# A hybrid encoder step on one core: the order of work around its search and attention, and where modulation rows are made

## The reference

```python
# A: gMLP over chunks of 128 tokens
u, v = split(gelu(za)); v = group_standardize(v)
a = u * (tril(w_spatial) @ v + b_spatial)
# B: attention on the 256 best keys of an indexer
score = sum_h(wi[h] * relu(qi[h] @ ki.T)); keep = top_k(score, 256)
b = softmax(q @ k.T / 8, over keep) @ v       # 8 heads on 2 key heads
# C: gated convolution of width 31, standardize, silu
x = x + ga1 * (concat(a, b, c) @ w_out)
x = x + ga2 * ((silu(h2 @ w_gate) * (h2 @ w_up)) @ w_down)
```

## Time and profile before

| | |
|---|---|
| median of 3 runs | 3089.64 us (3088.87 to 3091.21) |
| profiled execution | 3094.46 us, span 3092.7 us, mean granted clock of TensorE 0.961 |
| TensorE, matmul | 2847.1 us busy (92%) |
| VectorE | 1653.3 us (53%) |
| ScalarE | 985.8 us (32%) |
| GpSimd | 617.6 us (20%) |
| DMA | 224.93 MB, mean 73 GB/s |

### The profile page before, as it was taken

How to read it: one execution, slowest core, us unless ns; L and a number is a source line. 1 busy time by engine, 2 the same in 40 slices (tenths; PEclk the granted TensorE clock), 3 DMA queues, 4 the chain that set the end, 5 groups by cost and what they waited for, 6 DMA issues and landing times.

```text
span 3092.7 us, 42630 instructions
## 1 busy us (share of the span) xinstructions
PE 2847.1 (92%) x15994; PEld 2459.7 (80%) x16018; DVE 1653.3 (53%) x2788; ACT 985.8 (32%) x1259; POOL 617.6 (20%) x262
## 2 busy tenths in 40 slices
PE   5999778969999999999979987889999999999996
PEld 2778633349999999999967875333899999999996
DVE  6758766684352443534544778564335435353355
ACT  4246536523221111111233563563332111111112
POOL 1411300001122222222242122000112222222221
PEclk9999889979999999999989998999899999999998
DMA  5412100142122222222241311001112222222222
GB/s 212 134 63 83 35 21 1 38 168 75 66 83 70 82 71 86 80 70 82 70 141 43 116 49 36 1 1 34 56 55 88 70 80 78 72 88 70 80 80 85
DMA packets 71351, 224.93 MB, mean 73 GB/s; under 512 B 17232, under 2 KB 17488, under 8 KB 70096
## 3 DMA queue, kind: packets, MB, share of 16 engines
q1 hardware_dynamic: 69664, 217.26, 21.1%
q10 hardware_dynamic: 1584, 6.29, 0.5%
HBM read 211.44 MB, written 11.54 MB: 72 GB/s over the span
## 4 chain that ended last, share of the span: by engine, by line
issue 46%; PE 36%; DVE 6%; ACT 5%; POOL 4%; DVEq 2%; DMA 1%; ACTq 0%; POOLq 0%; SPq 0%
PE ps L919 33%; ACT notsel L728 4%; POOL w_lo L581 4%; PE ps L965 1%; DVE hf L1311 1%; DMA w_ada<-in_w_ada 1%; DVEq L1436 1%; PE ps L1026 1%; DVE ada_later L1330 1%; DVE ada_junk L1330 0%; PE ps L945 0%; DVE s_cand L1434 0%; DVE swapped L1401 0%; DVEq L1340 0%; PE ps L903 0%
## 5 line engine op out<-in xcount | busy, mean ns | idle before, releaser
L581 POOL TENSOR_TENSOR w_lo<-w_raw,w_hi 128x1024 fp32r<-128x1024 f32 x202 | 498.3, 2467 | 2360.6 <-ACT w_hi L680 2360.6
L919 PE MATMUL ps<-u_hi,w_hi 128*128 128x352 f32 (+1 forms) x2112 | 457.4, 325 | 2.1 <-ACT rstd L872 2.1
L919 PE MATMUL ps<-u_hi,w_lo 128*128 128x352 f32 (+1 forms) x2112 | 458.4, 325 | 0.0
L919 PE MATMUL ps<-u_lo,w_hi 128*128 128x352 f32 (+1 forms) x2112 | 455.7, 324 | 0.0
L680 ACT CAST w_hi<-w_raw 128x1024 fp32r<-128x1024 f32 x202 | 211.0, 1045 | 545.7 <-PE ps L919 336.1
L919 PEld LDWEIGHTS ps<-u_hi,w_hi 128*128 128x128 f32 x2112 | 362.1, 189 | 3.7 <-ACT rstd L872 2.7
L919 PEld LDWEIGHTS ps<-u_hi,w_lo 128*128 128x128 f32 x2112 | 361.0, 189 | 0.0
L919 PEld LDWEIGHTS ps<-u_lo,w_hi 128*128 128x128 f32 x2112 | 361.0, 189 | 0.0
L728 ACT ACTIVATE notsel<-score,s_cand 128x384 bf16<-128x384 f32 (+3 forms) x248 | 297.4, 1200 | 142.2 <-DVE s_cand L1434 141.9
L1741 DVE SCALAR_TENSOR_TENSOR x<-ps,mod,x 128x704 f32 (+2 forms) x240 | 125.4, 578 | 364.5 <-PE ps L919 358.8
L919 PE MATMUL ps<-a_hi,w_hi 128*128 128x352 f32 x1056 | 228.8, 325 | 4.2 <-POOL w_lo L581 2.1
(11 more groups left out here) (260 smaller groups left out, 4122.9 us busy)
## 6 DMA issues: line engine op xcount, KB each, us to landing
w_ada<-in_w_ada SPq DMA_DIRECT2D x96, 512.0 KB, 4.6
w_raw<-in_w_up SPq DMA_DIRECT2D x88, 512.0 KB, 3.5
w_raw<-in_w_in SPq DMA_DIRECT2D x34, 512.0 KB, 3.6
ada_later<-in_w_ada SPq DMA_DIRECT2D x32, 512.0 KB, 3.5
cw<-in_convw SPq DMA_DIRECT2D x32, 512.0 KB, 4.5
w_raw<-in_w_down SPq DMA_DIRECT2D x32, 384.0 KB, 3.1
w_raw<-in_w_down SPq DMA_DIRECT2D x32, 320.0 KB, 2.9
w_raw<-in_w_out SPq DMA_DIRECT2D x16, 512.0 KB, 3.5
```

Of the source, the lines that this page charges most:

```text
L581: nc.gpsimd.tensor_tensor(w_lo[slot][:], w_raw[:], w_hi[slot][:].bitcast(F32), ALU.subtract)\
L919: last = nc.tensor.matmul(ps[:, bank + t, 0:w], wt[slot][:, kk, :], mv[:, kk, t * TW:t * TW + w], start=(kk == 0 and p == 0), stop=(kk == ...
```

## The change

At the start TensorE makes eight groups of modulation rows in place of twelve, VectorE eight in place of four; both of VectorE's loads are on SP's queue, TensorE's on ScalarE's. `ADA_AT` is 3, 3, 1, 3, ten in all, and the later part is twelve and ten; SP loads them three at a time. `pv` of a unit is issued behind the next unit of `ORDER`, whichever kind it is. In `SEARCH_BESIDE` rounds ScalarE's count stands behind the exponentials. ScalarE's `turned(0)` stands in front of the last prompt search round; VectorE has gate rows 0, then `q_samp`, then `finish_search`, gate rows 1, the last `scale`, and both selects. SP loads strip 18 (`FIRST_OUT + 1`) directly behind the cached values. `output(QB)` stands in front of `modulation(l, 1, 2, 6)`.

```diff
@@ -108,11 +108,11 @@
 TILE = TOK * 4
-ADA_PE, ADA_DVE = 3, 1
+ADA_PE, ADA_DVE = 2, 2
...
 ADA_SLOTS = 3
-ADA_AT = {0: 2, 1: 2, 2: 2, 3: 2}
+ADA_AT = {0: 3, 1: 3, 2: 1, 3: 3}
 ADA_STRIPS = sum(ADA_AT.values())
@@ -418,7 +418,9 @@
             sp.dma_start(cond_row[:], a["cond_row"]).then_inc(row_loaded.sem, 16)
-            sp.dma_start(w_ada0[0][:], a["w_ada"][DEPTH - 1, 4 * ADA_PE:ADA_FIRST].rearrange("m p k -> p m k")).then_inc(ada0_loaded[0].sem, 16)
+            for n in range(ADA_DVE):
+                m = 4 * (ADA_PE + n)
+                sp.dma_start(w_ada0[n][:], a["w_ada"][DEPTH - 1, m:m + 4].rearrange("m p k -> p m k")).then_inc(ada0_loaded[n].sem, 16)
@@ -466,7 +468,7 @@
                     if l == 0 and 3 <= j <= 5:
-                        load_later(2 * j - 3, min(2 * j - 1, ADA_STRIPS))
+                        load_later(3 * j - 6, min(3 * j - 3, ADA_STRIPS))
                     if j == S_QI1:
@@ -531,18 +533,18 @@
                     sp.dma_start(vcache[:, :, n, 0:HD], a["vcache"][l, :, :, n]).then_inc(kv_cached.sem, 16)
+                load_strip(FIRST_OUT + 1, a["w_out"][l, 1])
                 if l == 0:
...
                         bring_back(d)
-                for j in range(1, OUT_STRIPS):
+                sp.wait_ge(c_ready.sem, c_ready.at(l, 2))
+                settle(sp)
+                for d in range(4, KD):
+                    bring_back(d)
+                for j in range(2, OUT_STRIPS):
                     load_strip(FIRST_OUT + j, a["w_out"][l, j])
-                    if j == 1:
-                        sp.wait_ge(c_ready.sem, c_ready.at(l, 2))
-                        settle(sp)
-                        for d in range(4, KD):
-                            bring_back(d)
@@ -695,7 +697,8 @@
             for n in range(ADA_PE):
-                act.dma_start(w_ada0[1 + n][:], a["w_ada0"][4 * n:4 * n + 4].rearrange("m p k -> p m k")).then_inc(ada0_loaded[1 + n].sem, 16)
+                act.dma_start(w_ada0[ADA_DVE + n][:], a["w_ada0"][4 * n:4 * n + 4].rearrange("m p k -> p m k"))\
+                    .then_inc(ada0_loaded[ADA_DVE + n].sem, 16)
             act.wait_ge(consts_made.sem, 1)
@@ -747,6 +750,14 @@
                     last.then_inc(st_rstd.sem, 1)
+
+                def turned(m):
+
+                    act.wait_ge(vn_turned.sem, vn_turned.at(l, m + 1))
+                    if m == 1:
+                        act.wait_ge(sp_ready.sem, sp_ready.at(l, 1))
+                    nc.scalar.copy(vnat[:, 0:QB, :], ps[:, 6:8, :])
+                    nc.scalar.copy(vnat[0:DEC, QB, :], ps[0:DEC, 5, 0:P]).then_inc(vn_ready.sem, 1)
@@ -787,18 +798,15 @@
                         square_centred(STATS_IN[j + 1])
+                    if j == IN_STRIPS - 1:
+                        turned(0)
                     if j in SEARCH_AFTER:
...
-                for m in range(2):
-                    act.wait_ge(vn_turned.sem, vn_turned.at(l, m + 1))
-                    if m == 1:
-                        act.wait_ge(sp_ready.sem, sp_ready.at(l, 1))
-                    nc.scalar.copy(vnat[:, 0:QB, :], ps[:, 6:8, :])
-                    nc.scalar.copy(vnat[0:DEC, QB, :], ps[0:DEC, 5, 0:P]).then_inc(vn_ready.sem, 1)
+                turned(1)
                 act.wait_ge(vaug_ones.sem, vaug_ones.at(l, 1))
@@ -827,10 +835,10 @@
                             searched += 1
+                    exponentials(t, P, PLACE["S", t], 512)
                     if kb < SEARCH_BESIDE.get(i, 0):
...
                         searched += 1
-                    exponentials(t, P, PLACE["S", t], 512)
                     if kb == i:
@@ -938,12 +946,12 @@
             for n in range(ADA_PE):
-                pe.wait_ge(ada0_loaded[1 + n].sem, 16)
+                pe.wait_ge(ada0_loaded[ADA_DVE + n].sem, 16)
                 if n >= 2:
...
                     last = nc.tensor.matmul(ps[0:2, n % 2, :], cond[:, kk, :],
-                                            w_ada0[1 + n][:, :, kk * P:(kk + 1) * P],
+                                            w_ada0[ADA_DVE + n][:, :, kk * P:(kk + 1) * P],
                                             start=(kk == 0), stop=(kk == KD - 1))
@@ -1167,16 +1175,16 @@
+                late = None
                 for kind, n in ORDER:
...
                         logits(n)
-                        continue
-                    st(n)
-                    i, kb = S_UNITS[n]
-                    if kb >= 1:
-                        pv(n - 1)
-                    if kb == i:
-                        pv(n)
+                    else:
+                        st(n)
+                    if late is not None:
+                        pv(late)
+                    late = n if kind == "S" else None
+                pv(late)
@@ -1383,10 +1391,11 @@
-            dve.wait_ge(ada0_loaded[0].sem, 16)
-            for e in range(4):
-                modulate(w_ada0[0][:, e], 4 * ADA_PE + e)
-                dve.drain()
+            for n in range(ADA_DVE):
+                dve.wait_ge(ada0_loaded[n].sem, 16)
+                for e in range(4):
+                    modulate(w_ada0[n][:, e], 4 * (ADA_PE + n) + e)
+                    dve.drain()
             cos = cossin[:, 0, :]
@@ -1595,12 +1604,9 @@
                             nc.vector.tensor_copy(score[0:DEC, s0:s0 + w], ps[0:DEC, 7, 0:w]).then_inc(samp_taken.sem, 1)
-                    if j == S_Q3:
-                        dve.wait_ge(kv_rot.sem, kv_rot.at(l, 5))
-                        nc.vector.tensor_copy(q_samp[:].rearrange("p (b t) -> p b t", b=4), q[:, :, SEQ:TOK])
                     if j == 8:
                         turn_input(1)
-                    if j in STATS_IN:
+                    if j in STATS_IN and j < S_Q3:
                         scale(STATS_IN[j])
@@ -1616,11 +1622,7 @@
-                finish_search(0, PSRCH)
-
-                assert searched == BITS
-
-                for m in range(2):
+                def gate_rows(m):
@@ -1634,6 +1636,14 @@
                     nc.vector.tensor_tensor(mix[:, m, :], mix[:, m, :], gu[:, m, :], ALU.mult).then_inc(gated.sem, 1)
+
+                gate_rows(0)
+                dve.wait_ge(kv_rot.sem, kv_rot.at(l, 5))
+                nc.vector.tensor_copy(q_samp[:].rearrange("p (b t) -> p b t", b=4), q[:, :, SEQ:TOK])
+                finish_search(0, PSRCH)
+                gate_rows(1)
+                scale(STATS_IN[S_Q3])
+                for m in range(2):
                     select(m, rank).then_inc(sel_ready.sem, 1)
@@ -1709,7 +1719,7 @@
                         diagonals(i + 1)
-                half = ADA_STRIPS + (48 - ADA_FIRST - ADA_STRIPS) // 2
+                half = ADA_STRIPS + 12
                 output(QB - 2, 2, P, (QB - 2) * P, (QB - 1) * P)
@@ -1725,8 +1735,9 @@
                     modulate_later(half, 48 - ADA_FIRST)
+                output(QB, 3, DEC, SEQ, TOK)
+                if l == 0:
                     modulation(l, 1, 2, 6)
-                output(QB, 3, DEC, SEQ, TOK)
                 for kk in range(KD):
```

## The result

The changed kernel takes 3095.93 us (median, 3091.97 to 3098.53) where the kernel before took 3090.22 in the same comparison: a ratio of 1.0017, 95% interval 1.0009 to 1.0024, so 5.7 us slower. The forecast was 3095.4. Its traced execution, though, took 3091.97 us, the lowest of all its times, and that of the kernel before 3094.46, near its highest.

The account below looks back on a forecast made before the run. Feed-forward halves and later output strips keep TensorE above 99%; in attention it waits for exponentials beside the search chains. Terms -3.2 + 7.1 - 5.6 + 7.45 = +5.75, added to the median 3089.64, give 3095.4 us; range 3080 to 3106.

Parts of the forecast that it names:

- The start: Up to the first strip: TensorE loses its third group, VectorE gets four more rows, `hf` starts at 54.7; -3.2 us.
- The forecast collision: At the start: a VectorE row piece beside POOL's split takes 3.3 us instead of 1.2, so VectorE ends at 53.7.
- Ten rows: Layer 0's first strips: ten modulation rows instead of eight, strip 4's wait grows from 4.98 to 12 us; +7.1 us.
- The gate stage: Between last input strip and attention: no wait at `q_samp`, first `smax` at 405.4 instead of 408.25; -2.85 us per layer.
- Attention: Late sums queue behind `select`, delaying reciprocals and the next block's first count; +7.45 us per layer, gate stage's gain included.
- The low clock: In attention, behind waits before block 4's logits and block 7's scores: TensorE's clock falls, costing 2.7 and 1.5 us.
- Layer 0's end: Ten rows instead of twelve, strip 18 loaded early, `output(QB)` first: cast at 683.65 instead of 689.22; -5.6 us, attention included.
- Rival C: Attention: low clock behind both long waits in both layers, +8.95 and -4.1, sum +8.75, 3098.4 us; 27%.
- Rival B: Attention: no low clock at all, +3.25 and -9.8 in layer 0, sum -2.65, 3087.0 us; 20%.
- Rival A: Attention: first counts don't wait for the moved sums, search follows TensorE's pace; -44.9 in all, 3044.7 us; 8%.

Follow-up runs that it names:

- rows_2222: The changed kernel with eight modulation rows (2, 2, 2, 2) behind the first input strips instead of ten, twelve before the sample tokens' output: 3094.68 us, ratio 1.0013.
- own_sums: The changed kernel with each unit of weighted sums issued where the kernel before issued it: 3053.14 us, ratio 0.9879.
- gate_old: The changed kernel with the gate stage in its old order: 3099.13 us, ratio 1.0030.

## Why the prediction was right, point by point

- **The start, -3.2**: -3.3 between the second traces, -4.6 between the first ones; undoing it costs 3.1 to 3.7 at the first strip. The number fits partly by luck, since two terms failed against each other. The forecast collision didn't happen: the row piece was under way when the split began, so VectorE was done at 50.60 and not at 53.7. By the Trainium skill (SBUF — State Buffer, Who interferes with whom) it is the order of issue that decides who waits, and the trace agrees: the piece kept 1.22 us, the split took 2.84 instead of 2.34. And the 1.5 us between the copy and `hf` that were to fall away stayed: it is 2.6 us from 50.75 to 53.34, as it was before, because the split now lay there.
- **Ten rows, +7.1**: the wait of 12.00 us is the forecast's 12. The stage grew by 4.9 us between the second traces, by 7.4 from `rows_2222` to the changed kernel, and by 6.6 between the means of all traces, inside the bounds of 4.9 and 9.3. That the later strips let the lag through was assumed; on the whole they do, but the second trace of before, with 2.3 us more of waiting at strip 4 and no longer strips, shows that a lag of that size can also vanish.
- **The gate stage, -2.85 per layer**: from strip 16's last matmul to the first `smax` the first traces show -1.0 and -1.7, the second ones -1.7 and -3.1. So the term was somewhat too large, by an amount that two traces of one kernel also differ by. Two things were missed. The last round, made sooner, has its decision beside POOL's rotation and split (377.73 to 382.46), where before it stood between the two: two operations of 0.17 us took 1.16 and 2.23. And the products took 5.37 us for the 4.3 forecast, with the clock at 0.57 from 376 to 380 (6.77 in the second trace). In layer 1 they took 3.72 us in one trace and 5.38 in the other, with the first `smax` at 34.3 us both times, so there they don't decide.
- **Attention, +7.45 with the gate stage**: up to strip 17 layer 1 shows +7.7 between the second traces and +6.6 between the first. Of the +7.7, 5.6 lie before the last weighted sums (264.8 to 270.4) and 2.1 behind, among the sample tokens, where nothing was forecast and the granted clock is 0.74 instead of 0.81; why it is lower there stays open. The mechanism can be followed block by block. Counted from the first `smax`, the scores of blocks 2 to 6 begin 2.8 us sooner and then 3.8, 5.1, 5.4 and 5.9 later in layer 0's second traces; the forecast had 1.1 sooner and 2.8, 4.5, 5.3 and 6.1 later. The waits for `select` were forecast as about 5, 2, 2, 2 and are 3.94, 1.16, 1.59, 1.76; the one before block 7's scores as 4.1 and is 3.11. The low clock was put behind two waits; the trace has four such stretches in layer 0. That the total comes so close is partly luck: waits that were somewhat too long and a gate stage that gave somewhat less stand beside a clock that fell more often and the 2.1 us behind the last sums.
- **Layer 0's end, -5.6**: -5.8. The named causes are all there: strip 18 waited for nothing, ten rows instead of twelve (4.8 by `rows_2222`), and `output` of block 6 later. That the load costs nothing where it now lies holds; what it was worth was left inside the sum, and is about 8 us.
- **The forecast of 3095.4** was set against the median, not the traced execution, and the measured 3095.93 lies 0.5 from it, closer than its own terms came. Rival C (3098.4) isn't excluded by the median alone. Its condition, low clock behind both long waits, is even met in layer 0 of both traces; its price of 8.95 us in layer 1 is not (7.7 and 6.6). Rival B has no low clock, and there is. Rival A is out for this kernel; but its figure of 3044.7, for a search that follows TensorE, is near what `own_sums` reached (3053.14) by leaving the sums where they were. The text named this condition and gave it 8% for a change in which late sums and early exponentials come together; it didn't see that one of the two could be had without the other.

What stays open: 1.8 us between the second traces lie in stages that the change leaves alone, and can't be told from chance by two traces. Strips 0 to 16 of layer 0 differ by 2 to 3 us between traces with the same work in them, and nothing here says why. Why the 1.5 us by which layer 1's first `smax` is later in `gate_old` are gone at the end of its attention wasn't settled. And it wasn't tried whether the late sums would pay with a search that ends earlier.

## What to carry to other kernels

An instruction moved "one unit later" to hide a wait is moved behind whatever the next unit waits for; before doing it, list what is queued behind its result on the other engines. Here one unit of weighted sums slid behind `select`, and reciprocals, output and the first count of the next search round slid with it: 20 us per layer. When two edits aim at the same wait, make each alone: the order of two ScalarE instructions removed the wait, and the second edit only had its price. And compare kernels by stages and with more than one trace each: two traces of one kernel differed here by 4 us in all, with a change of 5.7, and one stage by up to 3.

## What the runs showed of the hardware

- TensorE's clock fell beside shorter waits than those on which the prediction counted, and the same wait did not always bring it down. In attention of the changed kernel the granted clock was 0.50 to 0.77 in stretches beside single waits of 1.87, 3.94, 2.47 and 3.11 us (rows above). In `own_sums` a wait of 2.85 us stands at the same place in both layers: layer 0 stayed at full clock, layer 1 fell to half behind it. Below are the stretch of layer 0 in which the wait lies, that of layer 1 in which it ends, and its row in layer 1.

```profile
456.00:460.00 4.00, 1.44 (x4) 0.37 (x2) 3.68 (x5) 2.08 (x2) 0.00 (x0) 1.00 0.00 0
1944.00:1948.00 4.00, 3.37 (x10) 1.03 (x10) 2.37 (x5) 1.58 (x1) 0.00 (x0) 0.50 0.01 2
```

```profile
1944.63 2.08 PE L1142 MATMUL ps<-k,q 64*128 64x512 f32 x4 [2.85 <-DVE notsel L1509]
```

- An operation of 128 x 6 elements, 0.17 us alone, took 2.23 us when it met POOL's split. It ended with the split (380.12 to 382.46): here the length of the other engine's instruction counted, not its own.
- A row piece that began 0.57 us before the split was not slowed, one that began 1.22 us after it (92.12, split at 90.90) took 3.25 us.
